# First layer of a three-layer kernel: the low halves of strips 9, 10 and 11 are made by GpSimd in VectorE's place

## The reference

```python
def first_block(x, ...):
    for layer in range(2):
        hn = rmsnorm(x, norm[layer])
        if layer == 0:
            q, k, v, u = jnp.split(hn @ even_w_in, ...)      # 8 query heads, 2 key heads of 64; u 512 wide
            q, k = rmsnorm(q, q_norm), rmsnorm(k, k_norm)
            o_attn = swa_sink_attention(q, k, v, sinks)      # window of 128, softmax with a sink
            o_ssm = s5_mixer(u, a, b, c, d, log_dt, w_glu, b_glu)   # state space, gelu, sigmoid gate
            mixed = jnp.concatenate([o_attn, o_ssm], -1) @ even_w_out
        else:
            mixed = stick_breaking_attention(*jnp.split(hn @ odd_w_in, 3, -1)) @ odd_w_out
        x = x + mixed
        hn = rmsnorm(x, ffn_norm[layer])
        x = x + (silu(hn @ w_gate[layer]) * (hn @ w_up[layer])) @ w_down[layer]
    return x
```

## Time and profile before

| what | value |
|---|---|
| median of 3 runs | 1547.47 us (1547.29 to 1549.95) |
| profiled execution, time | 1546.95 us |
| profiled execution, span from first to last instruction | 1544.9 us |
| TensorE matmul busy | 1517.0 us, 98% |
| VectorE busy | 1237.8 us, 80% |
| ScalarE busy | 868.5 us, 56% |
| GpSimd busy | 234.2 us, 15%, 94 low halves among it |
| granted TensorE clock | 1.00 in every slice of the page |

### The profile page before, as it was taken

The page is one execution under the profiler, slowest core; times in us unless marked ns, Lnnn a source line. Parts: engine busy times, 40 slices in busy tenths (PEclk is TensorE's granted clock), DMA queues, the critical chain, the costliest instruction groups (busy, mean ns, idle before and its releaser), DMA issues.

```text
span 1544.9 us, 30295 instructions
## 1 busy us (share of the span) xinstructions
PE 1517.0 (98%) x10109; PEld 1315.6 (85%) x10109; DVE 1237.8 (80%) x2361; ACT 868.5 (56%) x1393; POOL 234.2 (15%) x101
## 2 busy tenths in 40 slices
PE   8899999999999999999999999999999999999999
PEld 8788888889888888988998888888888888878887
DVE  8978888745788887775899986999999999965555
ACT  7964434568744346665766566555554444444453
POOL 1010000145100001000678747100000000000000
PEclk9999999999999999999999999999999999999999
DMA  6145555543465655434445556555555555555654
GB/s 232 43 163 173 184 194 188 175 148 117 156 210 186 191 190 176 150 121 165 150 165 191 167 186 203 177 166 175 167 172 164 177 172 170 173 177 192 197 194 150
DMA packets 72493, 264.56 MB, mean 171 GB/s; under 512 B 8048, under 2 KB 8304, under 8 KB 72048
## 3 DMA queue, kind: packets, MB, share of 16 engines
q1 hardware_dynamic: 71712, 260.97, 51.3%
q10 hardware_dynamic: 720, 2.77, 0.5%
HBM read 262.66 MB, written 1.05 MB: 171 GB/s over the span
## 4 chain that ended last, share of the span: by engine, by line
PE 84%; DVE 11%; ACT 2%; issue 2%; DMA 0%; DVEq 0%; ACTq 0%
PE ps L748 34%; PE ps L604 21%; PE ps L608 11%; DVE arena L1896 4%; PE ps L572 3%; PE ps L576 3%; PE ps L573 3%; PE ps L1254 2%; PE ps L662 1%; DVE w_lo L1896 1%; DVE arena L2566 1%; DVE arena L2567 1%; DVE arena L2569 1%; DVE arena L2568 1%; ACT w_hi L1345 1%
## 5 line engine op out<-in xcount | busy, mean ns | idle before, releaser
L1345 ACT ACTIVATE w_hi<-ring 128x1024 fp32r<-128x1024 f32 x489 | 515.4, 1057 | 347.0 <-PE ps L748 207.8
L1896 DVE TENSOR_TENSOR w_lo<-ring,w_hi 128x1024 fp32r<-128x1024 f32 x395 | 481.3, 1220 | 59.5 <-ACT w_hi L1345 53.6
L604 PE MATMUL ps<-hT,w_hi 128*128 128x512 f32 x1696 | 427.1, 394 | 1.9 <-DVE arena L1896 0.9
L604 PEld LDWEIGHTS ps<-hT,w_hi 128*128 128x128 f32 x1696 | 307.1, 189 | 59.5 <-DVE arena L1896 1.6
L2810 POOL TENSOR_TENSOR w_lo<-ring,w_hi 128x1024 fp32r<-128x1024 f32 x94 | 229.1, 2444 | 739.8 <-DVE w_lo L1896 390.8
L748 PE MATMUL ps<-w_hi,halves_hi 128*128 128x512 f32 x688 | 271.7, 395 | 0.6 <-DVE halves_lo L1896 0.6
L748 PE MATMUL ps<-w_hi,halves_lo 128*128 128x512 f32 x688 | 268.7, 391 | 0.0
L608 PEld LDWEIGHTS ps<-hT,w_lo 128*128 128x128 f32 x1696 | 231.1, 190 | 17.4 <-DVE w_lo L1896 0.7
L608 PE MATMUL ps<-hT,w_lo 128*128 128x256 f32 x1696 | 236.6, 282 | 0.0
L748 PE MATMUL ps<-w_lo,halves_hi 128*128 128x512 f32 x688 | 185.4, 390 | 0.0
L748 PEld LDWEIGHTS ps<-w_lo,halves_hi 128*128 128x128 f32 x688 | 129.0, 188 | 27.9 <-DVE w_lo L1896 0.6
(11 more groups left out here) (360 smaller groups left out, 1808.5 us busy)
## 6 DMA issues: line engine op xcount, KB each, us to landing
ring<-in_strips SPq DMA_DIRECT2D x489, 512.0 KB, 3.4
const<-in_const SPq DMA_DIRECT2D x1, 1384.0 KB, 11.3
x_s<-in_x SPq DMA_DIRECT2D x2, 512.0 KB, 4.3
arena<-in_rel ACTq DMA_DIRECT2D x1, 1024.0 KB, 4.9
arena<-in_keys ACTq DMA_DIRECT2D x1, 1024.0 KB, 6.1
out<-x_s SPq DMA_DIRECT2D x4, 256.0 KB, 2.2
arena<-in_ssm_bc SPq DMA_DIRECT2D x1, 512.0 KB, 7.7
arena<-in_ssm_b SPq DMA_DIRECT2D x1, 512.0 KB, 8.4
```

The costliest lines, as they stand in the source:

```text
L604: pe.matmul(bank, w[0][:, c * P:(c + 1) * P], hT[:, c].rearrange("p s t -> p (s t)"), start=c == 0, stop=False, skip_group_check=True)
L1345: sc.activation(w_hi[:, n % RING, :], ring[:, n % RING, :], ACT.Copy).then_inc(high_ready, 1)
L1896: return ve.tensor_tensor(o, a, b, op)
```

## The change

VectorE no longer makes the low halves of strips 9, 10 and 11; GpSimd makes them, in a run of its own, after it has waited for the low half of strip 8 to be done. VectorE gets a wait ahead of strip 12's low half, for `low_ready` to reach 12, that is for GpSimd to be done with strip 11.

```diff
                 scores_in(0)
                 scores_in(1)
-                low(9)
                 scale_of(0)
...
                 scale_of(1)
                 y(0)
                 ssm(2)
-                low(10)
-                low(11)
                 for j in range(4):
                     ve.wait_ge(mix_high, j // 2 * 2 + 2)
                     tt(hT_lo[:, EVEN_SLOTS[j], :], ps[:, 6 + j // 2, (j % 2) * T:(j % 2 + 1) * T],
                        hT_hi[:, EVEN_SLOTS[j], :].bitcast(F32), ALU.subtract).then_inc(mix_low, 1)
+                ve.wait_ge(low_ready, AT[("even", "out", 2)])
                 low(12)
...
             po.memset(e_m[:, :, 0:1], 0.0).then_inc(zeroed, 1)

+            po.wait_ge(low_ready, AT[("even", "v", 0)])
+            lows(("even", "v", 0), ("even", "out", 1))
             po.wait_ge(low_ready, AT[("mlp0", "gate", 0)])
             lows(("mlp0", "gate", 0), ("mlp0", "up", 0))
```

## The result

The changed kernel is slower: 1555.09 us median of 14 runs (1550.88 to 1559.11), against 1547.55 for the kernel before (1547.13 to 1554.51, 14 runs). The ratio is 1.0033, with a 95% interval of 1.002 to 1.0046. The forecast was 0.26% slower, in a range of 0.03% to 0.41%: the measured 0.33% lies inside it, but the median of the 14 runs, 1555.09, lies above 1553.8, the upper end of the range in microseconds.

What follows compares the result with a forecast made beforehand. TensorE carries 84% of the chain, but VectorE's pace from 42 to 70 us moves everything behind it. The sum -0.47 + 2.21 + 2.21 = +3.95 us gave a median of 1551.4 us, range 1548.0 to 1553.8.

Steps and rivals of the forecast that it cites:

- Gain of 0.47 us: Without strip 9's low half on VectorE, ScalarE's scaling at 70.64 no longer waits; 0.47 us reaches TensorE.
- First meeting: Strip 9 on GpSimd blocks VectorE's second 128x768 product through the shared SBUF read port, near 44 us: 2.21 us lost.
- Second meeting: Strip 10 on GpSimd, asked for near 47.7 us, meets VectorE's next product, pushed there by the first delay: 2.21 us lost.
- Two meetings and not one: Main case: GpSimd gets turns between VectorE's back-to-back instructions, so strips 9 and 10 both cost 2.21 us; chance 0.64.
- The rival in which VectorE keeps the port: VectorE holds the port through back-to-back instructions; strip 9 costs 1.69 us, net +1.2 to +3.4 us; chance 0.20.
- the one in which GpSimd waits until 49.17: GpSimd loses every contest until VectorE's run ends, works beside the scores; only -0.47 us remains, 1547.0; chance 0.07.
- Strip 11 and the new wait ahead of strip 12: GpSimd ends strip 11 at 83.1, meeting no two-SBUF-input VectorE instruction; strip 12's low half waits for nothing.
- Who carries the delay: The 4.42 us delay before the scores moves all engines together; TensorE's out rows start 3.95 us after 79.73.
- Sum: Whole kernel: -0.47 + 2.21 + 2.21 = +3.95 us, median 1551.4, 0.26% slower.
- third effect on top of two meetings: Third meeting, strip 11 on `ssm(2)` or late strip 9, or slow GpSimd start: 2.2 us more, 1553.6; chance 0.07.

Runs made afterwards that it cites:

- strip 9 alone: Against the changed kernel, only strip 9's low half stays on GpSimd, strips 10 and 11 return to VectorE: 1549.59 us, ratio 1.0019 to the kernel before.
- VectorE late: Changed kernel with GpSimd's strips delayed to avoid meetings and three unused VectorE instructions added at two places: 1553.39 us, ratio 1.0032 to the kernel before.

## Why the prediction was right, and what it left out

- **Gain of 0.47 us.** Right in size and place. With the meetings avoided, it is all that is left (0.5 us in the times; from strip 8's low half to the out rows 37.07 us instead of 37.63, so 0.56), and ScalarE's wait ahead of the scaling is gone in every such profile.
- **First meeting, 2.21 us.** Measured: 3.14 for 0.95, 2.19 us, at the place and in the order foreseen.
- **Second meeting, 2.21 us.** Measured: 3.10 for 0.95, 2.15 us, on the second of the last four. That it would fall at the end of the run without the first meeting was argued from the rows; no run tests it.
- **Two meetings and not one.** The bound taken, that GpSimd gets its turn between instructions issued back to back, held in every profile that had such a meeting. The rival in which VectorE keeps the port is ruled out, and so is the one in which GpSimd waits until 49.17.
- **Strip 11 and the new wait ahead of strip 12.** Free: GpSimd has it at 83.22, strip 12's low half starts on VectorE at 84.16.
- **Who carries the delay.** The whole of it reached TensorE's out rows: 3.77 us from strip 8's low half on, where the sum had 3.95, and the three measured terms give 2.19 + 2.15 - 0.56 = 3.78. That the rows start at 83.78, so close to the 83.7 forecast, is in part luck, as 0.28 of it lies ahead of the change. At the full clock the kernel takes 1551.14 to 1551.25; the forecast was 1551.4.
- **Sum.** Here a term was missing. The sum took TensorE's clock as given, although the step on who carries the delay made TensorE wait longer in two places. The median of 14 is 1555.1 and not 1551.4 because two thirds of the runs lose 1.4 to 8 us more to a lower clock. That the ratio over all runs, 0.33% slower, still came out so close to 0.26% is partly luck: it would have been further off with a few more low runs, and the prediction has no reason for their number. The chance for a third effect on top of two meetings was put at 0.07, and with another cause.

What is shown of the clock: lateness of VectorE is enough to make low runs common (with no meeting, 8 of 12 low), and filling both pauses ended them (0 of 23, against 15 of 23 in the changed kernel; on one chip and beside each other, 0 of 12 against 6 of 9), while filling only the first did not (8 of 12, on the other chip). Filling only the second was not run, so it is not shown that the first has to be filled. What stays open is why some runs of one and the same kernel keep the clock and others lose it: with strip 9 alone the profile has the wait of 2.49 us and the full clock behind it.

## What to carry to other kernels

Before an elementwise instruction goes to GpSimd, look at what VectorE does at that time and not at how busy it is: a GpSimd instruction that reads SBUF and a VectorE instruction with two SBUF inputs run one after the other, so 2.4 us of GpSimd cost the chain 2.2. Placed beside VectorE instructions that read PSUM or have one SBUF input, the same work was free, and a wait on a counter put it there. And where a stall makes TensorE wait, read the granted clock of several executions and not one time: here two pauses of TensorE, 2.2 and 1.2 us longer than before, came with low runs that lost up to 8 us more, twice what the stall itself cost.

## What the runs showed that I had not expected

One kernel's runs fall roughly into groups by the granted clock (1551.1, 1553, 1555.1, 1557.4 and 1559 us for the changed kernel), and a single profile may come from any of them: the changed kernel's first profile shows the half clock for some 3.4 us, hidden behind VectorE, its second one for about 10 us. A low clock may fall elsewhere too: the profile with strip 9 alone has 0.66 in the stretch from 340 to 345 us, in the second layer, and its time was 1549.17, in the full group; the profile with VectorE late has 0.71 there. So the clock can also fall far from the changed piece. Where it fell in the 17 low runs of the kernel before is not known, as none of them was profiled.

```profile
340.00:345.00 5.00, 5.00 (x30) 5.00 (x29) 1.92 (x2) 4.93 (x6) 4.33 (x2) 0.66 0.32 107
```
